# Feed-forward second product with seven-product blocks for four of eight row pairs, from separately loaded weight blocks

## The reference

```
x = x + merged(conv branch, latent attention branch) @ w_out
x = x + memory_cross_attention(rms_norm(x), rms_norm(mem))
x = x + square(relu(rms_norm(x) @ w_ff1)) @ w_ff2      # 2048 -> 8192 -> 2048
out = rms_norm(x)
```

## Time and profile before

| | |
|---|---|
| median of 3 runs | 1606.21 us (1606.19 to 1606.55) |
| span of the profiled execution | 1604.8 us |
| TensorE (PE) matmul busy | 1595.9 us, 99% |
| VectorE (DVE) busy | 1252.5 us, 78% |
| ScalarE (ACT) busy | 866.1 us, 54% |
| GpSimd (POOL) busy | 75.9 us, 5% |
| moved by DMA | 304.97 MB, mean 190 GB/s |

### The profile page before, as it was taken

The page is one execution under the profiler, slowest core; times in us unless marked ns, Lnnn a source line. Parts: engine busy times, 40 slices in busy tenths (PEclk is TensorE's granted clock), DMA queues, the critical chain, the costliest instruction groups (busy, mean ns, idle before and its releaser), DMA issues.

```text
span 1604.8 us, 22691 instructions
## 1 busy us (share of the span) xinstructions
PE 1595.9 (99%) x7962; PEld 1352.9 (84%) x7962; DVE 1252.5 (78%) x1681; ACT 866.1 (54%) x1120; POOL 75.9 (5%) x160
## 2 busy tenths in 40 slices
PE   9999999999999999999999999999999999999998
PEld 8888888888888888888888888888888888888886
DVE  5588889999989898786887665885677666866587
ACT  7444456555555556754566655454464455545555
POOL 6500010000000000000000000000000000000001
PEclk9999999999999999999999999999999999999999
DMA  7665645555555665556664566666666666666555
GB/s 256 203 192 184 196 151 171 177 176 174 184 171 170 210 207 181 200 183 238 210 197 138 164 186 191 201 198 190 190 211 196 182 185 196 197 197 187 192 187 182
DMA packets 161294, 304.97 MB, mean 190 GB/s; under 512 B 11689, under 2 KB 20513, under 8 KB 160801
## 3 DMA queue, kind: packets, MB, share of 16 engines
q1 hardware_dynamic: 160128, 300.45, 58.9%
q0 software_dynamic: 1056, 3.46, 0.6%
q10 hardware_dynamic: 32, 0.01, 0.0%
HBM read 301.78 MB, written 2.10 MB: 189 GB/s over the span
## 4 chain that ended last, share of the span: by engine, by line
PE 98%; DVE 1%; DMA 1%; issue 0%; ACT 0%; SPq 0%; ACTq 0%; POOL 0%; DVEq 0%; POOLq 0%
PE ps L2255 15%; PE ps L1750 12%; PE ps L1752 12%; PE ps L1751 12%; PE ps L2025 9%; PE ps L2024 9%; PE ps L2023 9%; PE ps L2257 7%; PE ps L1763 1%; PE ps L1929 1%; PE ps L2146 1%; PE ps L1932 1%; PE ps L1914 1%; PE ps L1913 1%; PE ps L1912 1%; DMA raw<-in_w_ff_dram 1%
## 5 line engine op out<-in xcount | busy, mean ns | idle before, releaser
L1079 DVE TENSOR_TENSOR w_both<-raw,w_both 128x1024 fp32r<-128x1024 f32 x538 | 656.6, 1223 | 257.0 <-ACT w_both L624 255.3
L624 ACT ACTIVATE w_both<-raw 128x1024 fp32r<-128x1024 f32 x538 | 568.7, 1060 | 527.7 <-PE ps L1752 181.7
L2255 PE MATMUL ps<-a_both,w_both 128*128 128x512 f32 x1024 | 321.9, 396 | 0.0
L1750 PE MATMUL ps<-w_both,a_both 128*128 128x512 f32 x636 | 252.4, 397 | 0.1
L1752 PE MATMUL ps<-w_both,a_both 128*128 128x512 f32 x636 | 248.3, 390 | 0.0
L1751 PE MATMUL ps<-w_both,a_both 128*128 128x512 f32 x636 | 248.2, 390 | 0.0
L2257 PEld LDWEIGHTS ps<-a_both,w_both 128*128 128x128 f32 x1024 | 192.5, 188 | 45.2
L1140 DVE SCALAR_TENSOR_TENSOR acc<-hconv,cwk,acc 128x256 f32<-128x256 f32 x464 | 205.1, 497 | 7.4 <-PE ps L1968 7.4
L2257 PE MATMUL ps<-a_both,w_both 128*128 128x256 f32 x1024 | 201.4, 278 | 0.0
L2023 PE MATMUL ps<-w_both,c_hi 128*128 128x512 f32 x504 | 196.7, 390 | 0.3 <-DVE w_both L1079 0.3
L2025 PE MATMUL ps<-w_both,c_lo 128*128 128x512 f32 x504 | 196.4, 390 | 0.0
(11 more groups left out here) (377 smaller groups left out, 1920.3 us busy)
## 6 DMA issues: line engine op xcount, KB each, us to landing
raw<-in_w_ff_dram SPq DMA_DIRECT2D x256, 512.0 KB, 4.1
raw<-in_w_in_dram SPq DMA_DIRECT2D x144, 512.0 KB, 3.6
raw<-in_w_mla_out_dram SPq DMA_DIRECT2D x32, 512.0 KB, 3.7
raw<-in_w_conv_out_dram SPq DMA_DIRECT2D x32, 512.0 KB, 4.3
raw<-in_w_out_dram SPq DMA_DIRECT2D x32, 512.0 KB, 4.5
raw<-in_w_ukv_dram SPq DMA_DIRECT2D x16, 512.0 KB, 3.8
raw<-in_w_xkv_dram SPq DMA_DIRECT2D x16, 512.0 KB, 4.0
raw<-in_w_uq_dram SPq DMA_DIRECT2D x16, 384.0 KB, 3.3
```

The source lines that it names most:

```text
L624: act.activation(whi[:, s, :], raw[:, s, :], ACT.Copy).then_inc(hi_ready, 1)
L1079: dve.tensor_tensor(wlo[:, s, :], raw[:, s, :], whi[:, s, :].bitcast(F32), ALU.subtract).then_inc(lo_ready, 1)
L1750: pe.matmul(sum_, x_hi[:, k0 + k, tok], w_hi, start=(first and k == 0), stop=False)
L2255: pe.matmul(both, whi[:, s, cols[n]], a_both[:, :, k0 + k, :], start=(first and k == 0), stop=False)
```

## The change

In the feed-forward second product:

- Four of the eight row pairs of each column pair are done with seven products, instead of two. The order of units is new (`FF_ORDER`, `LAST_ORDER`), with left units at places 2, 5, 8, 11 and right units at 3, 6, 9, 12 (in the last pair 2, 5, 8, 10 and 3, 6, 9, 11).
- The blocks for the weight sums no longer come from the ring. For each such row pair one more load of 1 MB (`load_blocks`) brings all four blocks to one of three places (`SLOTS`). VectorE makes the sums in place (`t_sums`) and ScalarE and VectorE split them (`t_high`, `t_low`), 2048 elements at a time. When is written in tables: `T_LOAD_FF1` and `T_PREP_FF1` for blocks 0 to 2 in the first product, `T_LOAD` and `T_PREP` for blocks 3 to 7. Of a right unit only its second half is loaded.
- A right unit does its own product and the four with weight sums at once. The sums of products go to banks of their own, so all eight banks are in use in a pair.
- ScalarE copies one bank to `m_sum`, VectorE forms two sums of banks (`m_sums`, four operations of 512), and adds both to `xres` (`add_m_sum`, `add_m_neg`). They replace `add_copies`, `add_ones` and `add_last`. `add_chunk(p, 0)` moves from step 14 to step 15, behind `m_sums`. `gain(2)` moves from step 13 to step 15 of the last pair.
- The activation sums are made for two chunks, in the first product's chunks 1 and 2.
- GpSimd waits until TensorE is done with all right units but the last (`m_done`) before it loads the final gain.

```diff
+FF_ORDER = ((1, 8), (0, 8), (0, 0), (1, 0), (0, 10), (0, 2), (1, 2), (0, 12), (0, 4), (1, 4),
+            (1, 10), (0, 6), (1, 6), (0, 14), (1, 12), (1, 14))
+FF_LEFT, FF_RIGHT = (2, 5, 8, 11), (3, 6, 9, 12)
+LAST_LEFT, LAST_RIGHT = (2, 5, 8, 10), (3, 6, 9, 11)
+T_LOAD_FF1 = {(0, 5): 0, (1, 2): 1, (2, 2): 2}
+T_PREP_FF1 = {(0, 6): 0, (1, 4): 1, (3, 4): 2}
+T_LOAD = {(0, 10): 3, (0, 13): 4, (1, 0): 5, (1, 3): 6, (1, 10): 7}
+T_PREP = {(0, 8): 3, (0, 11): 4, (1, 1): 5, (1, 4): 6, (1, 8): 7}
...
+            def load_blocks(g, j):
+                p, m = j // FM, j % FM
+                src = w_ff2[:, ds(g * KT + 2 * m, 2), 2 * NC * p:2 * NC * (p + 1)]
+                if j < SLOTS:
+                    sp.wait_ge(chunk_out, g * CH + N_FF)
+                else:
+                    sp.wait_ge(m_done, g * FJ + (j - SLOTS + 1))
+                sp.dma_start(t_raw[j % SLOTS][:].rearrange("p (k c) n -> p k (c n)", k=2), src).then_inc(t_landed[j % SLOTS], 16)
...
-            pool.wait_ge(ws_lo_ready, 4 * SEVENS)
+            pool.wait_ge(m_done, FJ * GROUPS - 1)
...
+            def t_high(g, j):
+                act.wait_ge(t_made, g * (3 * FJ) + 3 * (j + 1))
+                act.activation(t_hi[j % SLOTS][:], t_raw[j % SLOTS][:], ACT.Copy).then_inc(t_hi_ready, 1)
...
+            def t_sums(g, j):
+                t, done = t_raw[j % SLOTS], 3 * j
+                dve.wait_ge(t_landed[j % SLOTS], ...)
+                dve.tensor_tensor(t[:, T1:T3 + 1, :], t[:, B11:B12 + 1, :], t[:, B12::2, :], ALU.add).then_inc(t_made, 1)
...
+                dve.tensor_tensor(t[:, T2, :], t[:, B22, :], t[:, T1, :], ALU.add).then_inc(t_made, 1)
...
+                dve.tensor_tensor(t[:, T4, :], t[:, B21, :], t[:, T2, :], ALU.add).then_inc(t_made, 1)
+            def t_low(g, j):
+                dve.wait_ge(t_hi_ready, g * FJ + (j + 1))
+                dve.tensor_tensor(t_lo[j % SLOTS][:], t_raw[j % SLOTS][:], t_hi[j % SLOTS][:].bitcast(F32), ALU.subtract).then_inc(t_lo_ready, 1)
...
+            def m_sums(g, p):
+                dve.wait_ge(y_copied, g * 2 + (Y_COPIED_FF + p + 1))
+                dve.wait_ge(m_done, g * FJ + FM * (p + 1))
+                ... four operations of 512 on the banks M6, M5, M7 and m_sum, m_neg
...
                     for k in range(FF2_UNITS):          # VectorE, second product, pair p
                         i = k + LEAD
+                        if (p, k) in T_PREP:
+                            t_sums(g, T_PREP[p, k])
+                        if (p, k - 1) in T_PREP:
+                            t_low(g, T_PREP[p, k - 1])
+                        if k == 15:
+                            dve.wait_ge(used, r + (U_FF + u + c0_done))
+                            add_chunk(p, 0)
                         if i in right:
                             lo_second(U_FF + u + i, r)
                         elif not last or u + i < FF_UNITS:
                             lo(U_FF + u + i, r)
-                        if k == right[1] + 2:
-                            dve.wait_ge(p4_done, g * 2 + (p + 4))
-                            add_chunk(p, 0)
-                        if k == right[1] + 3:
-                            add_copies(g, p, g * CH + (N_FF + 2 * p + 1))
-                            add_ones(g, p)
-                            add_last(g, p)
-                        if k == 13 and ends:
+                        if k == right[-1] + 2:
+                            m_sums(g, p)
+                        if k == 15:
+                            add_m_sum(g, p)
+                            add_m_neg(g, p, ends)
+                        if k == 15 and ends:
                             gain(2)
...
+                    elif i in right:                    # TensorE
+                        pe.wait_ge(h_lo_ready, g * 2 + (m // 2 + 3))
+                        into(banks[1], combined(3, m), slot(i, 1), i).then_inc(used, 1)
+                        pe.wait_ge(t_lo_ready, g * FJ + (FM * p + m + 1))
+                        into(m6, combined(1, m), weight_sum(T2, m), i)
+                        into(banks[0] + 1, hidden(2 * m + 1, 1), weight_sum(T4, m), i)
+                        into(m5, combined(0, m), weight_sum(T1, m), i)
+                        into(m7, combined(2, m), weight_sum(T3, m), i).then_inc(m_done, 1)
```

More of the change, by code:

```diff
@@ L304, in build @@
         ff_row = at(o, "ff_row", [P, 2, CPB, SEQ])
+        m_sum = at(o, "m_sum", [P, TT, NC])
+        m_neg = at(o + nbytes([P, TT, NC]), "m_neg", [P, TT, NC])
         pT = at(o, "pT", [P, 2, SW])
@@ L2025, in product, with seven_pair @@
                 return pe.matmul(ps[:, bank, :], x_lo, w_hi, start=False, stop=last, skip_group_check=True)
-            def seven_pair(g, p, u, r, banks, first_use, between, sums, b=late, x_hi=c_hi, x_lo=c_lo, order=FF2_ORDER, left=LEFT, right=RIGHT):
+            def seven_pair(g, p, u, r, banks, first_use, between, sums, b=late, x_hi=c_hi, x_lo=c_lo):
                 def hidden(k, t):
@@ L2243, in last_units, with stream_pair, hidden, combined @@
+                        pe.matmul(to, c_hi[:, k, tok], w_lo, start=False, stop=False, skip_group_check=True)
+                        mm = pe.matmul(to, c_lo[:, k, tok], w_hi, start=False, stop=(k == KT - 1), skip_group_check=True)
                     mm.then_inc(tail_used, 1)
+            def stream_pair(g, p, u, r, order, left, right, first_use):
+                banks = FF2_BANKS[p]
+                m1, m6, m5, m7 = M1_BANK, M6_BANK[p], M5_BANK[p], M7_BANK
+                def hidden(k, t):
+                    tok = slice(P * t, P * (t + 1))
+                    return c_hi[:, k, tok], c_lo[:, k, tok]
+                def combined(n, m):
+                    return fh_hi[m // 2][:, n, m % 2, :], fh_lo[m // 2][:, n, m % 2, :]
+                def slot(i, half):
+                    cols = slice(NC * half, NC * (half + 1))
+                    return whi[:, (u + i) % RING, cols], wlo[:, (u + i) % RING, cols]
+                def weight_sum(n, m):
+                    s = (FM * p + m) % SLOTS
+                    return t_hi[s][:, n, :], t_lo[s][:, n, :]
+                final = {}
+                for i, (c, k) in enumerate(order):
+                    if i in left:
+                        final[m1], final[banks[0]] = i, i
+                    elif i in right:
+                        for bank in (banks[1], m6, banks[0] + 1, m5, m7):
+                            final[bank] = i
+                    else:
+                        final[banks[c]], final[banks[c] + 1] = i, i
+                begun = set()
+                def into(bank, x, w, i, ends=True):
+                    mm = product(bank, *x, *w, first=bank not in begun, last=ends and final[bank] == i)
+                    begun.add(bank)
+                    return mm
+                for i, (c, k) in enumerate(order):
+                    if order is LAST_ORDER and i == FF2_UNITS - 4:
+                        last_units()
+                        break
+                    pe.wait_ge(lo_ready, u + i + 1 + r)
+                    first_use(i, c, k)
+                    if i in left:
+                        m = left.index(i)
+                        mm = into(m1, hidden(2 * m, 0), slot(i, 0), i)
+                        if m == FM - 1:
+                            mm.then_inc(y_step, 1)
+                        into(banks[0], hidden(2 * m + 1, 0), slot(i, 1), i).then_inc(used, 1)
+                    elif i in right:
+                        m = right.index(i)
+                        pe.wait_ge(h_lo_ready, g * 2 + (m // 2 + 3))
[5 more added lines that the diff above has]
+                        into(m7, combined(2, m), weight_sum(T3, m), i).then_inc(m_done, 1)
+                    else:
+                        for n in range(2):
+                            for t in range(TT):
+                                mm = into(banks[c] + t, hidden(k + n, t), slot(i, n), i, n == 1)
+                        mm.then_inc(used, 1)
```

227 lines of the change are left out of this document (164 added, 63 removed).

## The result

The changed kernel takes 1615.42 us (median of 4 runs, 1613.76 to 1616.34) beside 1606.38 us for the kernel before; the ratio is 1.0055, 95% interval 1.0042 to 1.0068. It is slower by 9.0 us; 7.7 were forecast. The profiled span is 1614.4 us, 9.6 above the span before.

The account below looks back on a forecast made before the run. TensorE, 99% busy, was taken to bound the kernel, with VectorE as the feeder to watch. -10.9 + 11.5 + 4.2 + 2.9 = +7.7 us on 1606.2 gave 1613.9 us, own range 1608 to 1620, with rivals 1598 to 1622.

Parts of the forecast that it names:

- What the change takes out: Feed-forward second product: 60 instead of 62 block products a pair, 48 matmuls at 0.2267 us, 10.9 us less.
- Durations without a row: 2048-element splits of weight-sum blocks, costed from 512 and 1024 forms: VectorE low part 2.29 us, ScalarE high part 1.92.
- The order, step by step: Walk of VectorE's stream in second pairs: late work holds TensorE 3.83 us per second pair, three groups, +11.5 us.
- the three behind low parts: Second-pair holds of TensorE waiting for VectorE's late low parts after blocks 5, 6 and 7: 1.33, 1.11, 0.35 us.
- the one at the banks: Next first product waits for banks 2 and 3, freed by chunk 0's add queued behind four sums: 1.04 us.
- The last pair: End of the last second product: holds of 1.33, 1.11 and, at place 11, 1.79 us, together +4.2.
- 1.33 + 1.11 too: Last pair assumed to have the same two holds as other second pairs, behind blocks 5 and 6.
- The tail: After the last matmul: VectorE's final adds and gain products, slowed beside GpSimd, delay the last tile, +2.9 us.
- Transfers at nothing: 24 MB of extra loads costed at zero: some 245 GB/s needed against 377 GB/s at the kernel's start.
- Rival C: Block loads land late, block 7 at 26.9 instead of by 24.4 us: +10 over four pairs, 1624; chance 0.10.
- The rule on shared ports: Tail: two-SBUF-input VectorE and SBUF-reading GpSimd instructions block each other outright, making the sum 0.3 us higher.
- The range: Own range 1608 to 1620 us, from eleven holds at 0.5 us either way plus the tail; with rivals 1598 to 1622.

Follow-up runs that it names:

- run 3: Changed kernel with block splits one step later and sums of banks plus chunk 0's add earlier, same instructions and loads: 1599.28 us, ratio 0.9962.
- run 9: Changed kernel with block splits later, bank sums earlier, three blocks in the last pair, and GpSimd's final gain loaded and multiplied earlier: 1596.11 us, ratio 0.9938.
- run 1: Changed kernel with ScalarE's and VectorE's split of each block one step later, a ring unit in front of each: 1603.99 us, ratio 0.9985.
- run 5: Changed kernel with one sum per block instead of three, the two 512-element sums left out (wrong weights): 1601.89 us, ratio 0.9976.
- run 2: Changed kernel with the four sums of banks one step earlier and chunk 0's add before step 14's low part: 1610.71 us, ratio 1.0032.
- run 8: Changed kernel with splits later, bank sums earlier, three blocks in the last pair, and GpSimd's gain products held until VectorE's are done: 1598.34 us, ratio 0.9951.
- run 6: Changed kernel with one extra 128 KB load into unused memory behind each of the 256 ring loads: 1624.22 us, ratio 1.0120.
- run 7: Kernel before the change with the same 256 extra 128 KB loads and the queue's loop written out: 1607.78 us, ratio 1.0013.

## Why the prediction was right, point by point

- **What the change takes out.** Right: 7914 matmuls instead of 7962, and 81.61 us for a second product where nothing holds it (run 3), which is 360 times 0.2267. The 10.9 us are real, and runs 3 and 9 collect most of them.
- **Durations without a row.** The 2048-element low part was put at 2.29 us and takes 2.29; the high part at 1.92 and takes 1.92. Two shorter forms of the same instruction were enough.
- **The order, step by step.** Right in place, releaser and size. Per second product 3.83 us of holds were forecast, and 85.58, 85.41 and 85.40 less 81.61 are 3.97, 3.80 and 3.79; over three groups 11.6 measured against 11.5 forecast. One by one, in group 1: 1.40, 1.10, 0.37 and 0.90 against 1.33, 1.11, 0.35 and 1.04. Runs 1 and 5 take away the three behind low parts and leave the one at the banks, run 2 does the reverse.
- **The last pair.** Sized too small: 86.74 and one matmul of 0.23 less 81.61 are 5.4 us against 4.2. The step that failed is "1.33 + 1.11 too": `LAST_ORDER` begins with chunk 0, and its banks are freed by an add that the forecast's own walk ends at 0.90. So TensorE waits at the very first unit (1.17 us from start to start), and of the hold at the sixth only 0.35 are left; the ninth has 1.13 and place 11 has 1.80, as forecast. A hold at the last ring unit (0.92) was not seen: its load was late and its low part ran beside GpSimd, 2.30 us instead of 1.23.
- **The tail.** 3.3 us against 2.9, but by another way; that the number fits is luck. The forecast had GpSimd beside VectorE's last adds. GpSimd ran from 1592.96 to 1599.00 and was through before those adds, the first of which starts at 1600.46. VectorE was late before them: its last low part ends 39.1 us after the second pair was due to start, where the forecast had 36.1, and the 1.99 us of waiting for the late load and 1.07 us beside GpSimd make up that difference.
- **Transfers at nothing.** Right for groups 0 to 2 (run 3), wrong at the end of the last pair, where a ring load landed after 7.9 us with the load of the final gain, which the change had moved, beside it. Whether the one made the other late is not shown. The reason given, peak rate, was too weak in any case: at 242 GB/s in the second products, far under the 377 of the earlier trace rows, the ring loads already landed after 4.5 us at the median instead of 4.1. What hid them was slack in the ring. Rival C, late block loads, did not happen: they land after 6.9 us at the median, and VectorE waited for one of them once in the feed-forward second products, 0.9 us.
- **The rule on shared ports** that the forecast weighed for the tail: the Trainium skill (SBUF — State Buffer, Who interferes with whom) has a VectorE instruction with two SBUF inputs blocked for a whole GpSimd instruction. Run 8 agrees: an instruction on 128x1 elements took 1.24 us instead of 0.15 beside GpSimd products of 1.4 us, which a mere lower rate could not do.
- **The range.** It counts eleven holds at 0.5 us either way; the table and the last pair have fifteen. The measured 1615.4 lies well inside either way.
- **Fit of the sum.** +7.7 forecast, +9.0 measured. The profiled executions differ by 9.6: second products 2.7 (forecast 3.3, of which the group 2 of before gives 0.6 back that it had lost by itself), last pair 2.6 (1.5), tail 3.3 (2.9), 0.9 outside.

## What to carry to other kernels

An engine that is busy for 83% can still be the last to be ready, when its list puts a long step in front of the one that is wanted; walk its list in program order against the times at which the bound engine wants each item, in the worst stretch, before judging by shares. A step that depends on a second engine should have other wanted work between its two halves, so that the reply comes in time (run 1: 11.4 us for four moved lines). Extra loads are free only while there is slack in the ring that takes them: the same 256 loads, with the waits that they bring to the queue, cost 1.6 us in one kernel and 8.8 in the other. The last load of a ring deserves a look of its own when another large load is moved beside it.

## What was not expected of the hardware

- A hold costs some 0.3 us more than the idle time in its row (1.10 shown, 1.40 from start to start), and a hold of 0.37 us has no idle time in its row at all; the first matmul behind it is shown with 0.50 instead of 0.39 us. Holds are to be measured from start to start.
- After 2.62 us without a matmul the granted clock was 0.50 in 1564.38 to 1566.00 (run 6); behind holds of up to 1.65 idle us it stayed at 1.00.
- Beside GpSimd's products of 1.4 to 1.5 us two very different instructions of VectorE, both with two SBUF inputs, take about 1.1 us longer: 1.24 us instead of 0.15 for 128x1 (run 8), 2.30 instead of 1.23 for 128x1024 (the changed kernel). The sums of banks, with one input in PSUM, keep their 0.68 us beside GpSimd (1596.51 in the changed kernel).
- The median landing of the 512 KB ring loads went from 4.1 to 4.5, 4.8 and 5.0 us as the mean rate in the second products rose from some 205 over 242 and 256 to 284 to 289 GB/s (before, after, runs 7 and 6), long before the rate of 377 GB/s that the core shows at the start.
